# A recurrent decoder trunk on one core: reordering the odd mixer's decay work, and moving four rank products inside their pieces

## The chip, the cores and the metric

The kernel runs on one core of a Trainium2 chip. The metric is the device time of one launch in microseconds (us), as a median over runs.

## The reference, cut to what matters

Two layers; each has a feed-forward half step, a mixer and a second feed-forward half step, for 512 prompt tokens and 8 samples of 8 tokens, all in float32. The even layer's mixer needs low-rank products whose sigmoids give decays. The odd layer's mixer joins a gated linear attention (GLA, "C") and an mLSTM ("D"), both of them chunked:

```python
def _gla(q, k, v, gk, s0):
    bc = jnp.cumsum(gk, -2)
    qd = q * jnp.exp(bc)
    att = jnp.where(causal, jnp.einsum('bnhik,bnhjk->bnhij', qd, k * jnp.exp(-bc)), 0.0)
    intra = jnp.einsum('bnhij,bnhjv->bnhiv', att, v)
    kd = k * jnp.exp(bc[..., -1:, :] - bc)
    # per chunk: o = in_c + qd_c @ s;  s = s * gl_c + kd_c^T v_c

def _mlstm(q, k, v, ig, fg, c0, n0, m0):
    # per chunk, with running maximum m_t:
    #   dm = exp(log_d - m_t) * (q k^T);  num = w_in * (q c) + dm v
    #   h = num / max(|den|, exp(-m_t));  ke = k * exp(log_e - m_new)

def _odd_mixer(h, s_gla, s_c, s_n, s_m, w, i):
    proj = h @ w['w_in_odd'][i]
    o_c = _rms(o_c) * gain_c * silu(z);  o_d = sigmoid(o_in) * _rms(hd) * gain_d
    return concat([o_c, o_d]) @ w['w_out_odd'][i], ...
```

## The kernel before, in words

The program is a sequence of blocks: a dense chain (first feed-forward, even projection), the even mixer, a long dense chain (even output, three feed-forward parts, odd projection), the odd mixer (`odd_mixer`, from L3461 on), and a last dense chain. All five engines run an order that is written out by hand; they meet at semaphores only, and each block ends on all of them before the next one begins.

**Dense chain.** Weights stream in 128-column tiles. Each tile is rounded into a high and a low part (ScalarE at L171, VectorE at L175), and TensorE forms three products per pair of tiles (L1494, L1496, L1498) over `KT` = 8 steps `kt` of the contracted dimension. One tile's worth of that is a piece. In the even projection's pieces numbered 19 to 23, small products for the even mixer are put in between (`even_gates.rank`, L761): after piece 19+i the product `w{i}`, in the middle of piece 20+i (at `kt == KT // 2`) the product `r{i}`. Both write the same PSUM pair, and ScalarE empties it each time with a sigmoid (`decay_rates`, L825): `r{i}` waits for `sig_w{i}`, `w{i+1}` for `sig_r{i}`.

**Odd mixer.** There are four prompt chunks of 128 tokens, 0 to 3, and one chunk of all samples (number 4). For each chunk c, by the names of the steps in `odd_orders` (L3405):

- TensorE: `front` transposes the values (`vct`, `vdt`, L3665), forms key-query products (`qk_0`, `qk_1`) and transposes the mLSTM keys (`kdt`, L3685); `weights` forms the GLA attention (`at_0`, `at_1`, whose 16x16, 32x32 and 64x64 blocks are separate products) and transposes the end-scaled keys (`klt`, L3721); `outputs` forms the outputs (`co`, `do`) and state updates (`sc`, `sd`); `back` transposes the normalised outputs back (`tc`, `td`, L3810). L3650 is the helper that records all plain products.
- ScalarE: `exponents` (L3847 to L3854: `X`, `Xn`, `xl`, `F`); `evict` copies the transposed values (`Vc` L3860, `Vd` L3863) and then computes the decay exponents of the mLSTM (`Lexp`, four at L3872, and `xw`, L3875); `keys` copies `klt` (`KL`, L3880); `square` (L3890) and `roots` (L3895, a square root, which needs another function table than the exponentials, so that ACT_TABLE_LOAD instructions come in between).
- VectorE: `front` (L3925 to L3942), `weights` (`qw` L3959, `DM` L3962, `KE` L3968), `masked` (`AT`, L3981), `sums` (L3996 to L4015), `scaled` (reciprocal L4019, `U` L4026), `gated` (L4062).
- GpSimd: `relative` (`rel`, six subtractions, L3554 and L3555, which `F` needs), `to_the_end` (`te`, L3567, which `xl` needs), `keys_to_end` (`Kl`, L3575), `end_decays` (`eC`, `eD`), and `masked_logs` (`lm`, L3606), which adds a causal mask to the rows of log decays that a DMA broadcast to all partitions; `Lexp` needs it.
- SP: broadcasts of the log rows of chunk 0 (L3514), of the entry rows that `xw` needs (L3517), of the log rows of chunks 1 to 3, each issued only when the one before has landed, then the samples' rows and the 2 MB of GLA and mLSTM states.

PSUM has four fixed banks for outputs and a ring of four for everything else: a job may start only when the fourth job before it in TensorE's order has been read out (`claim`, `odd_release`), so that the order itself sets which step waits for which.

## Time and profile before

| | before |
|---|---|
| median of 3 runs | 2659.85 us (2652.95 to 2662.24) |
| the profiled execution, its own time | 2658.36 us |
| span of its trace | 2656.6 us |
| TensorE busy | 2541.6 us (96%) |
| VectorE / ScalarE / GpSimd busy | 1604.7 / 1057.3 / 650.2 us |
| odd mixer, from 2078.5 to 2188.5 us of the span | 110 us |
| even projection's pieces with rank products, from 570.2 to 608.7 us | 38.5 us |

The span is the trace's own length; the execution's time is 1.8 us more, for what lies around it. Shares of busy time are means over the whole launch, so the odd mixer is read by itself.

### The profile page before, as it was taken

To read this page: it belongs to the slowest core of one execution; us is meant where nothing else is said; L and a number is where in the kernel's file an instruction comes from. 1 tells how busy PE (TensorE), PEld (TensorE's weight loads), DVE (VectorE), ACT (ScalarE), POOL (GpSimd) and SP (SyncE) were. 2 spreads that over 40 slices of the span, in tenths; PEclk is the share of its full clock that TensorE was granted. 3 is DMA by queue.
4 is the path that set the end of the run, shared out by engine and by line. 5 is a ranking of instruction groups with operands and counts; after the bars stand their busy time and mean duration, and the time that the engine had idled before them with its cause. 6 is when DMAs were issued, how large, how long until landed. Compare 5 with 4: busy or idle time off the path is not lost. (4 is left out here: it accounts for less than half of the span.)

```text
span 2656.6 us, 52472 instructions
## 1 busy us (share of the span) xinstructions
PE 2541.6 (96%) x22720; PEld 2389.8 (90%) x22720; DVE 1604.7 (60%) x2302; ACT 1057.3 (40%) x1546; POOL 650.2 (24%) x499
## 2 busy tenths in 40 slices
PE   6999999999999899999999999999999679999998
PEld 4999999888787787999999999999989569999998
DVE  5678726665465555677842677852743356677825
ACT  4444414554344322444432544432432333444513
POOL 0455201000010031155501055500100312355301
PEclk8999999999999979999999999999999789999999
DMA  6332455631000014222255322255751213222324
GB/s 238 104 120 95 157 192 193 236 131 54 29 3 3 9 60 163 64 95 93 93 194 177 121 90 96 96 183 175 234 200 60 76 52 105 66 94 96 101 83 133
DMA packets 82846, 303.30 MB, mean 114 GB/s; under 512 B 9376, under 2 KB 17072, under 8 KB 81336
## 3 DMA queue, kind: packets, MB, share of 16 engines
q1 hardware_dynamic: 82616, 299.95, 34.2%
q8 instruction: 179, 2.93, 0.4%
q14 instruction: 51, 0.42, 0.0%
HBM read 289.16 MB, written 10.76 MB: 113 GB/s over the span
## 5 line engine op out<-in xcount | busy, mean ns | idle before, releaser
L175 DVE TENSOR_TENSOR weights_r<-work,weights_r 128x1024 fp32r<-128x1024 f32 (+2 forms) x309 | 389.6, 1261 | 339.2 <-ACT weights_r L171 339.2
L171 ACT ACTIVATE weights_r<-work 128x1024 fp32r<-128x1024 f32 (+2 forms) x309 | 299.1, 968 | 534.0 <-PE banks L1498 298.9
L1379 POOL TENSOR_TENSOR rows<-rows,consts 128x288 f32<-128x288 f32 (+3 forms) x64 | 82.1, 1282 | 711.8 <-ACT consts L1641 711.8
L1496 PE MATMUL banks<-low_r,weights_r 128*128 128x288 f32 (+1 forms) x1064 | 255.3, 299 | 0.0
L1397 PE MATMUL banks<-big_r,weights_r 128*128 128x288 f32 x768 | 227.0, 296 | 0.0
L1398 PE MATMUL banks<-h_r,weights_r 128*128 128x288 f32 x768 | 226.6, 295 | 0.0
L1396 PE MATMUL banks<-h_r,weights_r 128*128 128x288 f32 x768 | 226.5, 295 | 0.0
L1494 PE MATMUL banks<-h_r,weights_r 128*128 128x288 f32 (+1 forms) x808 | 201.7, 307 | 4.7 <-DVE big_r L437 4.7
L1496 PE MATMUL banks<-big_r,weights_r 128*128 128x288 f32 (+2 forms) x800 | 202.0, 298 | 0.0
L175 DVE TENSOR_TENSOR ring_r<-consts,ring_r 128x1024 fp32r<-128x1024 f32 (+1 forms) x87 | 105.7, 1215 | 153.1 <-ACT ring_r L171 153.1
L1498 PE MATMUL banks<-h_r,weights_r 128*128 128x288 f32 (+1 forms) x808 | 195.3, 299 | 0.0
L1494 PE MATMUL banks<-low_r,weights_r 128*128 128x288 f32 (+2 forms) x720 | 182.1, 302 | 12.0 <-DVE low_r L175 12.0
L1496 PEld LDWEIGHTS banks<-low_r,weights_r 128*128 128x128 f32 x1064 | 181.5, 190 | 0.1
L1498 PE MATMUL banks<-low_r,weights_r 128*128 128x288 f32 (+2 forms) x720 | 178.9, 298 | 0.0
L1396 PE MATMUL banks<-low_r,weights_r 128*128 128x288 f32 x576 | 170.1, 295 | 0.0
L1397 PE MATMUL banks<-low_r,weights_r 128*128 128x288 f32 x576 | 169.9, 295 | 0.0
L1398 PE MATMUL banks<-low_r,weights_r 128*128 128x288 f32 x576 | 169.4, 294 | 0.0
L1494 PEld LDWEIGHTS banks<-h_r,weights_r 128*128 128x128 f32 x808 | 138.0, 190 | 24.3 <-issue 8.9
L171 ACT ACTIVATE ring_r<-consts 128x1024 fp32r<-128x1024 f32 (+1 forms) x87 | 89.6, 1030 | 170.0 <-PE banks L1498 152.4
L1494 PEld LDWEIGHTS banks<-low_r,weights_r 128*128 128x128 f32 x720 | 124.8, 191 | 23.1 <-DVE weights_r L175 13.0
L1398 PEld LDWEIGHTS banks<-h_r,weights_r 128*128 128x128 f32 x768 | 144.9, 189 | 0.0
L1397 PEld LDWEIGHTS banks<-big_r,weights_r 128*128 128x128 f32 x768 | 144.6, 188 | 0.0
(581 smaller groups left out, 7084.9 us busy)
## 6 DMA issues: line engine op xcount, KB each, us to landing
work<-w_ff_dram SPq DMA_DIRECT2D x117, 512.0 KB, 3.6
h<-w_mod_dram SPq DMA_DIRECT2D x48, 768.0 KB, 5.3
consts<-w_ff_dram SPq DMA_DIRECT2D x59, 512.0 KB, 3.6
work<-w_down_dram SPq DMA_DIRECT2D x55, 512.0 KB, 3.5
big_buf<-w_mod_dram SPq DMA_DIRECT2D x24, 768.0 KB, 6.1
consts<-w_down_dram SPq DMA_DIRECT2D x33, 512.0 KB, 3.5
work<-w_down_dram SPq DMA_DIRECT2D x33, 384.0 KB, 3.4
work<-w_mod_first_dram SPq DMA_DIRECT2D x24, 512.0 KB, 12.0
```

What stands on the lines that cost most here:

```text
L171: return act.activation(high, raw, ACT.Copy)
L175: return engine.tensor_tensor(low, raw, high.bitcast(F32), ALU.subtract)
L1379: pool.tensor_tensor(k.rows[:, c], k.rows[:, c], k.square[:, c], ALU.add).then_inc(added, 1)
L1396: pe.matmul(out, low[:, w], x_high, start=j == 0, stop=False)
L1397: pe.matmul(out, high[:, w], x_low, start=False, stop=False)
L1398: last = pe.matmul(out, high[:, w], x_high, start=False, stop=j == KT // 2 - 1)
L1494: pe.matmul(out[a], low[:, w], x[a][0], start=begins, stop=False)
L1496: pe.matmul(out[a], high[:, w], x[a][1], start=False, stop=False)
L1498: last = pe.matmul(out[a], high[:, w], x[a][0], start=False, stop=closes)
```

## The change

It has two parts. In the dense chain the four products `r0` to `r3` move from `kt == 4` to `kt == 6` of their pieces. In the odd mixer:

- ScalarE: `Lexp` and `xw` leave `evict` and become `log_exponents`, which follows `exponents` directly, ahead of `KL`, `root`, `Vc` and `Vd`. At the start `Vc` and `Vd` of chunk 0 come first of all.
- GpSimd: `lm` of a chunk moves from ahead of `rel` (and one chunk early) to behind `te` of its own chunk.
- TensorE: `weights` of chunk 0 moves ahead of `front` of chunk 1.
- VectorE: `masked` of chunk 0 and `front` of chunk 1 come ahead of `weights` of chunk 1.
- SP: each log row has a semaphore of its own, and none is held back for the one before.

```diff
@@ -1471,7 +1471,7 @@
                         for kt in range(lo, hi):
-                            if even_gates and kt == KT // 2 and i in range(even_at(20), even_at(24)):
+                            if even_gates and kt == KT - 2 and i in range(even_at(20), even_at(24)):
                                 even_gates.rank(pe, "r", i - even_at(20))
@@ -3407,7 +3407,8 @@
     front_act = lambda c: pick(c, "X Xn xl F", "X Xn xl")
-    weight_act = lambda c: at(c, ["Vc", "Vd"] + [f"Lexp_{h}" for h in range(2 if c == SAMPLE else 4)] + ["xw"])
+    log_act = lambda c: at(c, [f"Lexp_{h}" for h in range(2 if c == SAMPLE else 4)] + ["xw"])
+    value_act = lambda c: at(c, ["Vc", "Vd"])
     square_act = lambda c: pick(c, "sqC_0 sqC_1 sqD_0 sqD_1", "sqC sqD")
@@ -3417,23 +3418,22 @@
     of = lambda i, names: names(ODD_ORDER[i]) if i < len(ODD_ORDER) else []
-    masks_pool = lambda i: of(i, lambda c: at(c, ["lm"]))
-    pe = of(0, front_pe) + of(1, front_pe) + of(0, weight_pe)
-    act = of(0, front_act) + of(0, weight_act) + of(1, weight_act) + at(ODD_ORDER[0], ["KL"]) + of(1, front_act)
-    dve = of(0, front_dve) + of(0, weight_dve) + of(1, weight_dve) + of(0, masked_dve) + of(1, front_dve)
-    pool = masks_pool(0)
+    pe = of(0, front_pe) + of(0, weight_pe) + of(1, front_pe)
+    act = of(0, value_act) + of(0, front_act) + of(0, log_act) + of(1, front_act) + at(ODD_ORDER[0], ["KL"]) \
+        + of(1, log_act) + of(1, value_act)
+    dve = of(0, front_dve) + of(0, weight_dve) + of(0, masked_dve) + of(1, front_dve) + of(1, weight_dve)
+    pool = []
     for i in places:
         c = ODD_ORDER[i]
-        pool += masks_pool(i + 1)
         if c != SAMPLE:
...
         pe += of_sample(i + 1, "sc0 sc1") + (out_pe(SAMPLE) if of_sample(i + 1, "co") else [])
-        act += square_act(c) + of(i + 2, front_act) + of(i + 1, lambda b: at(b, ["KL"])) + at(c, ["root"]) \
-            + of(i + 2, weight_act)
+        act += square_act(c) + of(i + 2, front_act) + of(i + 2, log_act) + of(i + 1, lambda b: at(b, ["KL"])) \
+            + at(c, ["root"]) + of(i + 2, value_act)
         dve += sums_dve(c) + of(i + 1, masked_dve) + scaled_dve(c) + of(i + 2, front_dve) + of(i + 2, weight_dve)
         dve += of_sample(i, "SC2 SC3 SD2 SD3 SD4 SD5") + gated_dve(c) + of_sample(i + 1, "SC0 SC1 SD0 SD1")
-        pool += pick(c, "rel te Kl eC eD", "te Kl eC eD KEm KLm")
+        pool += pick(c, "rel te lm Kl eC eD", "te lm Kl eC eD KEm KLm")
     return pe, act, dve, pool
@@ -3490,7 +3490,8 @@
         states_in, cleared, n_ready = (ph.sem(x) for x in ("states_in", "cleared", "n_ready"))
-        logs_in, sample_logs_in, entries_in = (ph.sem(x) for x in ("logs_in", "sample_logs_in", "entries_in"))
+        sample_logs_in, entries_in = (ph.sem(x) for x in ("sample_logs_in", "entries_in"))
+        logs_in = [ph.sem(f"logs_in_{c}") for c in range(NCH)]
         log_of = lambda c: log_rows[:, c * 4 * n:(c + 1) * 4 * n].rearrange("p (h i) -> p h i", h=4)
@@ -3511,12 +3512,11 @@
                 def chunk_logs(c):
-                    sp.dma_start(log_of(c), log[None, :, c * n:(c + 1) * n].to_broadcast([P, 4, n])).then_inc(logs_in, 16)
+                    sp.dma_start(log_of(c), log[None, :, c * n:(c + 1) * n].to_broadcast([P, 4, n])).then_inc(logs_in[c], 16)
                 chunk_logs(0)
...
                 for c in range(1, NCH):
-                    sp.wait_ge(logs_in, 16 * c)
                     chunk_logs(c)
@@ -3599,10 +3599,12 @@
                         pool.wait_ge(sample_logs_in, 32)
+                        pool.wait_ge(constants.landed, 32)
                         tt(v2(log_rows_s), v2(log_rows_s), k.half("cut_below8")[:, None, :].to_broadcast([P, 2, m]), ALU.add)\
...
                         return
-                    pool.wait_ge(logs_in, 16 * (c + 1))
+                    pool.wait_ge(logs_in[c], 16)
+                    pool.wait_ge(constants.landed, 32)
                     tt(log_of(c), log_of(c), k.big("cut_below")[:, None, :].to_broadcast([P, 4, n]), ALU.add)\
@@ -3612,15 +3614,12 @@
                 last.then_inc(cleared, 1)
-                pool.wait_ge(constants.landed, 32)
-                masked_logs(ODD_ORDER[0])
                 for i in places:
                     c = ODD_ORDER[i]
-                    if i + 1 < len(ODD_ORDER):
-                        masked_logs(ODD_ORDER[i + 1])
                     if c != SAMPLE:
...
                     to_the_end(c, i)
+                    masked_logs(c)
                     keys_to_end(c, i)
@@ -3813,8 +3812,8 @@
                 front(ODD_ORDER[0])
+                weights(ODD_ORDER[0])
                 front(ODD_ORDER[1])
-                weights(ODD_ORDER[0])
                 for i in places:
@@ -3854,7 +3853,6 @@
                 def evict(c, i):
-                    w = size(c)
                     act.wait_ge(*after("pe", "vct", c))
@@ -3862,6 +3860,9 @@
                         .then_inc(*did("Vd", c))
+
+                def log_exponents(c, i):
+                    w = size(c)
                     act.wait_ge(*after("pool", "lm", c))
@@ -3894,16 +3895,19 @@
 
+                evict(ODD_ORDER[0], 0)
                 exponents(ODD_ORDER[0], 0)
-                evict(ODD_ORDER[0], 0)
+                log_exponents(ODD_ORDER[0], 0)
+                exponents(ODD_ORDER[1], 1)
+                keys(ODD_ORDER[0], 0)
+                log_exponents(ODD_ORDER[1], 1)
                 evict(ODD_ORDER[1], 1)
-                keys(ODD_ORDER[0], 0)
-                exponents(ODD_ORDER[1], 1)
                 for i in places:
...
                         exponents(ODD_ORDER[i + 2], i + 2)
+                        log_exponents(ODD_ORDER[i + 2], i + 2)
                     if i + 1 < len(ODD_ORDER):
@@ -4064,9 +4068,9 @@
                 weights(ODD_ORDER[0], 0)
-                weights(ODD_ORDER[1], 1)
                 masked(ODD_ORDER[0], 0)
                 front(ODD_ORDER[1], 1)
+                weights(ODD_ORDER[1], 1)
                 for i in places:
```

How the orders move, at the three places that matter. First ScalarE in the odd mixer, in the turn of chunk 1 (squares of chunk 1, exponents of chunk 3, key copy of chunk 2, root of chunk 1). Before:

```order
L3847 ACTIVATE work<-big_buf 128x512
L3849 ACTIVATE work<-big_buf 128x256
L3851 ACTIVATE work<-work 128x256
L3854 ACTIVATE work<-work 128x768
L3880 ACTIVATE work<-banks 128x256
L3895 ACT_TABLE_LOAD
L3895 ACTIVATE work<-work 128x8
L3860 ACTIVATE work<-banks 128x512
L3863 ACTIVATE work<-banks 128x4x128
L3872 ACT_TABLE_LOAD
L3872 ACTIVATE work<-work,cols 128x128 x4
L3875 ACTIVATE work<-work 128x256
```

and with the change:

```order
L3846 ACT_TABLE_LOAD
L3846 ACTIVATE work<-big_buf 128x512
L3848 ACTIVATE work<-big_buf 128x256
L3850 ACTIVATE work<-work 128x256
L3853 ACTIVATE work<-work 128x768
L3873 ACTIVATE work<-work,cols 128x128 x4
L3876 ACTIVATE work<-work 128x256
L3881 ACTIVATE work<-banks 128x256
L3896 ACT_TABLE_LOAD
L3896 ACTIVATE work<-work 128x8
L3858 ACTIVATE work<-banks 128x512
L3861 ACTIVATE work<-banks 128x4x128
```

The four `Lexp` and `xw` now stand ahead of the key copy and the root, and the load of the exponential's table has moved from between the root and `Lexp` to ahead of `X`.

Second, TensorE at the start of the odd mixer (`front` is the rows x8, x4, x2; `weights` the five rows on `work` up to 64x64 and the transposes after them). Before:

```order
L3665 MATMUL banks<-base,big_buf 128x128 x8
L3650 MATMUL banks<-big_buf 128x128 x4
L3685 MATMUL banks<-base,big_buf 128x128 x2
L3665 MATMUL banks<-base,big_buf 128x128 x8
L3650 MATMUL banks<-big_buf 128x128 x4
L3685 MATMUL banks<-base,big_buf 128x128 x2
L3650 MATMUL banks<-work 128x128 x4
L3650 MATMUL banks<-work 16x16 x16
L3650 MATMUL banks<-work 32x32 x8
L3650 MATMUL banks<-work 64x64 x4
L3721 MATMUL banks<-base,work 128x128 x2
L3650 MATMUL banks<-work 128x128 x2
```

and with the change:

```order
L3664 MATMUL banks<-base,big_buf 128x128 x8
L3649 MATMUL banks<-big_buf 128x128 x4
L3684 MATMUL banks<-base,big_buf 128x128 x2
L3649 MATMUL banks<-work 128x128 x4
L3649 MATMUL banks<-work 16x16 x16
L3649 MATMUL banks<-work 32x32 x8
L3649 MATMUL banks<-work 64x64 x4
L3720 MATMUL banks<-base,work 128x128 x2
L3664 MATMUL banks<-base,big_buf 128x128 x8
L3649 MATMUL banks<-big_buf 128x128 x4
L3684 MATMUL banks<-base,big_buf 128x128 x2
L3649 MATMUL banks<-work 128x128 x2
```

`weights` of chunk 0 now stands between the two fronts.

Third, TensorE in the even projection, the last of the four pieces with an `r` product (L761). Before:

```order
L1498 MATMUL banks<-h_r,weights_r 128x300 x2
L761 MATMUL banks<-big_buf,work 128x288 x2
L1494 MATMUL banks<-h_r,weights_r 128x300 x2
L1496 MATMUL banks<-low_r,weights_r 128x300 x2
L1498 MATMUL banks<-h_r,weights_r 128x300 x2
L1494 MATMUL banks<-h_r,weights_r 128x300 x2
L1496 MATMUL banks<-low_r,weights_r 128x300 x2
L1498 MATMUL banks<-h_r,weights_r 128x300 x2
L1494 MATMUL banks<-h_r,weights_r 128x300 x2
L1496 MATMUL banks<-low_r,weights_r 128x300 x2
```

and with the change:

```order
L1498 MATMUL banks<-h_r,weights_r 128x300 x2
L1494 MATMUL banks<-h_r,weights_r 128x300 x2
L1496 MATMUL banks<-low_r,weights_r 128x300 x2
L1498 MATMUL banks<-h_r,weights_r 128x300 x2
L1494 MATMUL banks<-h_r,weights_r 128x300 x2
L1496 MATMUL banks<-low_r,weights_r 128x300 x2
L1498 MATMUL banks<-h_r,weights_r 128x300 x2
L761 MATMUL banks<-big_buf,work 128x288 x2
L1494 MATMUL banks<-h_r,weights_r 128x300 x2
L1496 MATMUL banks<-low_r,weights_r 128x300 x2
```

The product stands two steps of `kt` (three products for two sides each) later in its piece.

## Rows read from the trace of the kernel before

**Rows 1.** The page: busy time, share of the span and instructions of the engines.

```profile
PE 2541.6 (96%) x22720; PEld 2389.8 (90%) x22720; DVE 1604.7 (60%) x2302; ACT 1057.3 (40%) x1546; POOL 650.2 (24%) x499
```

**Rows 2.** Waits, 569 to 612 us: engine, line, waited for; us in total, times, longest.

```profile
PE banks L761 <- ACT work L825: 4.3, 4, 1.1
```

**Rows 3.** Timeline, TensorE and ScalarE around `r0` and `w1`: start, us, engine, instruction, idle before.

```profile
575.19 0.74 ACT L825 ACTIVATE work<-banks,params 128x576 f32<-128x576 f32 x1
575.98 1.24 PE L761 MATMUL banks<-big_buf,work 64*128 64x288 f32 x4 [1.08 <-ACT work L825]
577.25 0.74 ACT L825 ACTIVATE work<-banks,params 128x576 f32<-128x576 f32 x1 [1.32 <-PE banks L761]
...
580.64 1.23 PE L761 MATMUL banks<-big_buf,work 64*128 64x288 f32 x4
```

**Rows 4.** Timeline, start of the odd mixer (begins at 2078.5 us).

```profile
2080.47 1.50 PE L3665 MATMUL banks<-base,big_buf 128*128 128x128 f32 x8 [4.04 <-DMA consts<-consts_in_dram]
...
2083.94 1.09 POOL L3606 TENSOR_TENSOR work<-work,consts 128x512 f32<-128x512 f32 x1 [2.89 <-DMA work<-decay_rows]
...
2088.71 0.40 POOL L3554 TENSOR_TENSOR work<-big_buf 128x128 f32<-128x128 f32 x1
...
2090.88 0.61 POOL L3567 TENSOR_TENSOR work<-big_buf 128x256 f32<-128x256 f32 x1
...
2092.57 0.58 ACT L3860 ACTIVATE work<-banks 128x512 f32<-128x512 f32 x1
...
2098.77 0.40 ACT L3875 ACTIVATE work<-work 128x256 f32<-128x256 f32 x1
...
2100.16 2.54 PE L3650 MATMUL banks<-work 64*128 64x128 f32 x64 [1.31 <-DVE work L3962]
...
2103.36 0.38 ACT L3880 ACTIVATE work<-banks 128x256 f32<-128x256 f32 x1 [4.19 <-PE banks L3721]
...
2103.84 1.19 PE L3650 MATMUL banks<-work 128*128 128x128 f32 x4 [0.52 <-DVE work L3981]
```

**Rows 5.** Timeline, SP's issue of the two entry rows (L3517).

```profile
2078.89 1.28 SPq L3517 DMA_DIRECT2D work<-decay_rows  x2
```

**Rows 6.** DMA issues, 2076 to 2100 us: KB of one, us from issue to landing.

```profile
work<-decay_rows SPq DMA_DIRECT2D x2, 288.0 KB, 5.7
...
work<-mn_in_dram SPq DMA_DIRECT2D x1, 8.0 KB, 8.4
```

**Rows 7.** Stretches: length, busy us of PE, PEld, DVE, ACT, POOL, clock, DMA share, GB/s.

```profile
2114.00:2118.00 4.00, 3.45 (x80) 2.74 (x76) 2.26 (x7) 2.00 (x4) 0.86 (x2) 0.86 0.01 4
```

```profile
2152.00:2153.00 1.00, 1.00 (x49) 0.78 (x48) 1.00 (x3) 0.00 (x0) 0.00 (x0) 0.66 0.00 0
```

**Rows 8.** Timeline, the turn of chunk 1, from the end of its squares to `td`.

```profile
2131.59 0.63 ACT L3847 ACTIVATE work<-big_buf 128x512 f32<-128x512 f32 x1
...
2132.72 0.84 ACT L3854 ACTIVATE work<-work 128x768 f32<-128x768 f32 x1
...
2134.63 0.38 ACT L3880 ACTIVATE work<-banks 128x256 f32<-128x256 f32 x1 [1.07 <-PE banks L3721]
...
2135.03 1.28 ACT L3895 ACT_TABLE_LOAD   x1
...
2138.82 1.28 ACT L3872 ACTIVATE work<-work,cols 128x128 f32<-128x128 f32 x4
...
2140.78 0.75 DVE L3962 SCALAR_TENSOR_TENSOR work<-banks,work 128x256 f32<-128x256 f32 x2
...
2141.34 1.09 PE L3810 MATMUL banks<-base,work 128*128 128x128 f32 x4 [3.07 <-DVE work L3962]
```

**Rows 9.** Timeline, ScalarE: key copies in the turns of chunks 0 and 2, root of chunk 3.

```profile
2115.97 0.38 ACT L3880 ACTIVATE work<-banks 128x256 f32<-128x256 f32 x1 [2.00 <-PE banks L3721]
...
2154.08 0.39 ACT L3880 ACTIVATE work<-banks 128x256 f32<-128x256 f32 x1 [3.02 <-PE banks L3721]
...
2166.64 0.21 ACT L3895 ACTIVATE work<-work 128x8 f32<-128x8 f32 x1 [0.92 <-DVE work L4015]
```

## The prediction

> **What bounds the kernel now.** First the page: TensorE is busy 96% of the span [rows 1], so time can only be won where TensorE idles or runs slowly. Neither edit removes a product. Next the waits of the stretch that each edit touches, then the timeline around them. In the even projection TensorE waits four times for a sigmoid of ScalarE, 4.3 us in all [rows 2]. In the odd mixer it idles between short bursts, and the stretches show the rest: the granted clock is at its lower level (0.50, 1.2 GHz against 2.4) until about 2115 us, and again in the turn of chunk 2 until 2152.7 (the 0.86 and 0.66 are means over a stretch with the change in it) [rows 7]. I read that part as a chain over all engines.
>
> **Even projection.** `r0` starts at 575.98 after 1.08 us of idling, right behind `sig_w0` (575.19 + 0.74 = 575.93); it would have been reached at 574.90 [rows 3]. From the end of `r0` (577.22) to `w1` (580.64) four steps of `kt` take 3.4 us, so two take 1.7, and `r0` is now reached at 576.6, 0.7 after the sigmoid. The wait goes: 4 x 1.07 = **-4.3 us** [rows 2]. A new wait could arise at `w1`, which needs `sig_r0`: that starts 1.27 after `r0` and takes 0.74 [rows 3], so it ends at 578.6, and `w1` comes at 576.6 + 1.24 + 1.7 = 579.5. With 0.9 us to spare it costs nothing. TensorE has no other wait there. Bounds: 0, if `w` waited as long as `r` did, and -4.3.
>
> **Start of the odd mixer.** Before, GpSimd waits 2.89 us for the first log row, masks it (1.09 us), then waits for and masks the second, and comes to `rel` only at 2088.71; `te` ends at 2091.49 [rows 4]. `xl` and `F`, the copies behind them and all of TensorE's work stand behind that; `at` of chunk 0 starts at 2100.16 and the first output product at 2103.84 [rows 4]. The new order, step by step:
>
> - `vct` and `vdt` end at 2081.97 (2080.47 + 1.50). `Vc` and `Vd`, 0.58 each, end at about 2082.6 [rows 4]. A table load of 1.28 follows, to 2083.9; `X` to `F` take 1.97 (2131.59 to 2133.56), to 2085.9 [rows 8].
> - `rel` and `te` take 2.78 (2088.71 to 2091.49). GpSimd is free at 2081.05, where its wait of 2.89 began, so `te` ends at 2083.8, in time for `xl`. The log row is there at 2083.94 and `lm` ends at 2085.0 [rows 4], in time for `Lexp`.
> - `Lexp` and `xw` take 1.28 + 0.40 less an overlap of 0.1, 1.6 in all [rows 4, 8], to 2087.5. The entry rows that `xw` needs are issued from 2078.89 and land 5.7 us after each issue, by about 2085.3 [rows 5, 6].
> - `at` followed the end of `xw` (2099.17) by 1.0 [rows 4]; it still does, through `DM`, which must empty a bank that `at_1` now claims. `at` starts at 2088.5.
> - `klt` was ready 3.2 after that start and `KL` 3.6 [rows 4]; so `klt` is ready at 2091.7. ScalarE first has `X` to `F` of chunk 1, whose `rel` and `te` start after `xw`: 2087.8 + 2.8 = 2090.6, `xl` and `F` to 2092.0, `KL` to 2092.4, `Lexp` and `xw` to 2094.0, `Vc` to 2094.5.
> - TensorE's front of chunk 1 is 1.5 for the transposes and 1.2 for `qk`, since four output products of that size take 1.19 at this clock [rows 4]: to 2094.4. `kdt`, half as many, waits for `Vc` and takes 0.6; outputs start at 2095.0.
>
> That is 2103.84 - 2095.0 = **-8.8 us**. Bounds: -5, if a wait of the size of those removed (2.9) and 0.9 of smaller ones come back, and -9.5. The four log rows now leave at once, ahead of 2 MB of states. I count nothing for that: the 8 KB row that was issued last, behind those 2 MB, took 8.4 us to land [rows 6], so later transfers queue behind earlier ones.
>
> **The turns.** In chunk 1's turn ScalarE goes from the squares through `X` to `F` (2133.56), waits 1.07 for `klt`, copies `KL`, loads the table and takes the root [rows 8]. Now a load (1.28) stands ahead of `X` and `Lexp` with `xw` (1.6) behind `F`: 2131.59 + 1.28 + 1.97 + 1.6 = 2136.4, against 2134.63: `KL` and the root come 1.8 later. Nothing is won behind the root: `xw` ended at about 2140.4 and `DM`, after a multiply of 0.4, started at 2140.78 [rows 4, 8], so VectorE came to it no earlier; it was busy from the root on. `td` waits for `DM` (3.07 idle) and the next outputs for `td` [rows 8], so this is on the path: **+1.8 us**. In chunk 0's turn there is no load ahead, and the 1.6 fit in ScalarE's 2.00 of idling; in chunk 2's the load and the half-size exponents, 1.28 + 0.8, fit in 3.02 [rows 9]. The root of chunk 3 waited for VectorE (0.92 idle), so the load that disappears there was hidden [rows 9]. Bounds: 0 if `klt` were later anyway, +5.4 if all three turns paid.
>
> Here a rule speaks for more. Rows first: a load takes 1.28 us and the next instruction follows at once [rows 8]. The Trainium skill, "ScalarE: Activation LUTs", *What ACT_TABLE_LOAD costs*, gives 1.28 plus a drain, 2.66 in all, and its *Table sets: the hidden batching unit* advises finishing one set before switching. The order has two loads fewer (8 to 6), which by that rule is -5.3 us; by rows it is nothing, since both removed loads were hidden.
>
> **Sum.** -4.3 - 8.8 - 1.4 + 1.8 = -12.7 us, so 2658.4 becomes 2645.7. The profiled execution is 1.5 below the median of its kernel, and for the median I forecast **2647 us**. A difference of 0.3% is 8 us; below that a measurement of this kernel tells nothing from no change.
>
> **Rivals.**
>
> - *Loads saved count.* By counting sets the two loads are 2 x 1.28 = 2.6 us more: 2644.5. For it: the order has them; against: ScalarE idles 3.02 and 0.92 where they stood [rows 9]. Chance 0.04. (The Trainium skill's batching rule, above, is this case.)
> - *Every turn pays.* If the clock's earlier return takes ScalarE's idling away, the turns of chunks 0 and 2 pay 1.8 too: +3.6, 2650.7. For it: only 0.4 to spare in one. Against: an earlier `klt` is itself a gain. Chance 0.08.
> - *The start gives half.* Some step that I have not seen, as a copy in ScalarE's order or a bank, takes up 3.8, and the clock comes back no earlier: -4.3 - 5 + 1.8 = -7.5, 2652.4. For it: ten steps in a row had to fit. Chance 0.10.
> - *Slower: the first log row is buried.* If transfers that are issued together share the engines evenly, the first log row and the entry rows land with the last. All in all they are 3.7 MB. The two 288 KB rows took 6.4 us (90 GB/s, with their latency), the last 2 MB of states 8.4 us (240 GB/s) [rows 5, 6]; at 160, between them, it is 23 us, landing near 2101.5. From there `lm`, `Lexp`, `xw` and on to the outputs are 1.1 + 1.6 + 1.0 + 6.5 = 10.2: outputs at 2111.7, +7.9. With -4.3 and +1.8: 2665.3. It decides from the point where that row lands after 2096. Against it: the 8.4 us [rows 6]. The Trainium skill, "DMA: Bandwidth & Descriptors", *Queues, rings and completion order*, says that each engine takes descriptors in ring order though completions may cross; with that the trace agrees. Chance 0.03.
> - *The change doesn't do what it says in the even part.* `w` inherits the wait: -8.4, 2651.5. Against: 0.9 us to spare. Chance 0.03.
>
> **How the numbers follow.** The forecast has 0.72. Its bounds run from -4.3 - 9.5 - 2.6 = -16.4 to -4.3 - 5 + 1.8 = -7.5, so 2643.5 to 2652.4; with 2 us of scatter on each side the range is 2641 to 2654.5, and it holds all rivals but the slower one. Faster by over 0.3%: 0.67 of the forecast, 0.04, 0.05 of the turns, 0.02 of the last, 0.78 in all. Within 0.3%: 0.05 of the forecast, 0.03, 0.10, 0.01, together 0.19. Slower: 0.03.
>
> **What would show it.** Right: no wait of TensorE at the rank products; outputs of chunk 0 near 16.5 us after the mixer's start, not 25.4; the clock back before 25 us; the root of chunk 1 6.5 us after the squares, not 4.7; the mixer 8 us shorter. Wrong: `xw` of chunk 0 waiting for a DMA, a new wait ahead of `kdt` or `at` of over 1 us, or the same mixer length with an earlier start, which would mean that a turn takes it back.

## The result, and the profile after

The changed kernel takes 2641.6 us (median of 6 runs, 2635.5 to 2643.8). The kernel before, run on the same occasions, takes 2654.1 (6 runs, 2651.1 to 2662.2). The ratio is 0.9946, with a 95% interval of 0.9927 to 0.9965: faster by 9 to 19 us, and in the middle by 14. The forecast was 2647 with a gain of 12.7.

The profiled executions differ by more, 2658.4 against 2641.6, since that of before lies 4.3 us above the median of its six runs and that of after lies on its own. The ledger below is of this pair. "Mixer" is the odd mixer, from its first memset (2078.46 before, 2073.90 after) to the first copy of the next dense chain (2188.53, 2171.38).

| stretch, us | before | after | change | forecast |
|---|---|---|---|---|
| `w0` to the even mixer's first product | 154.19 | 149.57 | -4.6 | -4.3 |
| mixer's start to first output product | 25.38 | 16.44 | -8.9 | -8.8 |
| first output to root of chunk 0 | 13.82 | 9.82 | -4.0 | -1.4 |
| root of chunk 0 to root of chunk 1 | 18.66 | 18.34 | -0.3 | +1.8 |
| root of chunk 1 to root of chunk 2 | 19.46 | 18.48 | -1.0 | 0 |
| root of chunk 2 to root of chunk 3 | 10.86 | 10.86 | 0 | 0 |
| root of chunk 3 to the mixer's end | 21.89 | 23.54 | +1.7 | 0 |
| the mixer | 110.07 | 97.48 | -12.6 | -8.4 |

The two blocks that were worked out in detail came as forecast. The rest of the mixer did not, and what is in it is the subject of the experiments. Below, turn 1 is the step from root of chunk 0 to root of chunk 1, and turn 2 the next one; each begins with the rest of the chunk before, up to its `td`.

The page's first part, which answers to [rows 1]:

```profile
PE 2534.6 (96%) x22720; PEld 2384.8 (90%) x22720; DVE 1604.1 (61%) x2302; ACT 1054.2 (40%) x1544; POOL 650.6 (25%) x499
```

TensorE has as many products as before and is busy 7.0 us less, since more of them ran at the higher clock; its idling (the span less the busy time) shrank from 115.0 to 105.3 us. ScalarE has two instructions fewer, the two table loads.

The timeline of the even projection, which answers to [rows 3] (columns as there):

```profile
575.44 0.74 ACT L825 ACTIVATE work<-banks,params 128x576 f32<-128x576 f32 x1
576.75 1.24 PE L761 MATMUL banks<-big_buf,work 64*128 64x288 f32 x4
578.02 0.74 ACT L825 ACTIVATE work<-banks,params 128x576 f32<-128x576 f32 x1 [1.83 <-PE banks L761]
579.74 1.24 PE L761 MATMUL banks<-big_buf,work 64*128 64x288 f32 x4
```

`sig_w0` ends at 576.18 and `r0` starts at 576.75 with no wait. `sig_r0` ends at 578.76 and `w1` starts at 579.74: the new spare time is 1.0 us (0.9 was reckoned), and `w` inherits nothing. From `w0` to `w1` a period is 9.33 us instead of 10.49.

The start of the odd mixer, which answers to [rows 4]:

```profile
2077.99 0.60 ACT L3861 ACTIVATE work<-banks 128x512 f32<-128x512 f32 x1 [0.26 <-PE banks L3664]
2078.61 1.28 ACT L3846 ACT_TABLE_LOAD   x1
2078.61 0.62 POOL L3567 TENSOR_TENSOR work<-big_buf 128x256 f32<-128x256 f32 x1
2079.18 1.10 POOL L3608 TENSOR_TENSOR work<-work,consts 128x512 f32<-128x512 f32 x1
...
2081.78 1.26 ACT L3873 ACTIVATE work<-work,cols 128x128 f32<-128x128 f32 x4
2082.95 0.40 ACT L3876 ACTIVATE work<-work 128x256 f32<-128x256 f32 x1
2084.29 2.54 PE L3649 MATMUL banks<-work 64*128 64x128 f32 x64 [4.55 <-ACT work L3848]
...
2090.34 0.61 PE L3649 MATMUL banks<-work 128*128 128x128 f32 x4
```

GpSimd goes from `te` to `lm` without waiting for the log row (L3608 at 2079.18, 5.3 after the start), and ScalarE goes through exponents and `xw` without waiting either. So the first log row wasn't buried behind the states, and `at` starts 10.4 after the mixer's start (forecast 10.0). The first output products take 0.61, not 1.19 as in [rows 4]: they already run at the higher clock.

The stretches say when it came back, and when it fell again. Columns: length, busy us of PE, PEld, DVE, ACT, POOL, then the granted clock, DMA share, GB/s.

```profile
2086.00:2088.00 2.00, 2.00 (x26) 1.82 (x19) 1.14 (x4) 1.37 (x4) 2.00 (x4) 0.50 1.01 303
2088.00:2090.00 2.00, 1.49 (x14) 1.12 (x12) 2.00 (x7) 2.00 (x8) 1.08 (x3) 0.91 0.54 147
2090.00:2094.00 4.00, 3.94 (x30) 3.16 (x30) 1.70 (x6) 1.15 (x4) 3.56 (x8) 1.00 0.01 0
...
2107.00:2109.00 2.00, 2.00 (x11) 1.55 (x12) 0.00 (x0) 0.00 (x0) 1.30 (x2) 0.54 0.00 0
2109.00:2112.00 3.00, 3.00 (x32) 2.39 (x34) 0.00 (x0) 1.17 (x4) 0.00 (x0) 1.00 0.00 0
...
2150.00:2152.00 2.00, 2.00 (x16) 1.67 (x17) 1.33 (x2) 0.00 (x0) 0.00 (x0) 0.50 0.22 41
```

The 2 us from 2088 are a mean of 0.91: 0.36 us of them were still at half the clock, so the change from 1.2 to 2.4 GHz lies at 2088.4, 14.5 after the mixer's start and 4.1 after the start of `at`. Before it was 36.7 and 15.0. In the turns the lower level returns: in turn 1 for 6.8 us, where before it stayed for 10.2, and in turn 2 for 13.7 in both. The last row is in the sample's outputs, where the clock was low for 3.4 us; before it wasn't: that is the +1.7 of the table.

The turn of chunk 1, which answers to [rows 8]:

```profile
2112.17 1.28 ACT L3846 ACT_TABLE_LOAD   x1
2114.01 0.44 PE L3720 MATMUL banks<-base,work 128*128 128x128 f32 x2
2116.52 0.40 ACT L3876 ACTIVATE work<-work 128x256 f32<-128x256 f32 x1
2116.82 0.36 ACT L3881 ACTIVATE work<-banks 128x256 f32<-128x256 f32 x1
2117.20 1.28 ACT L3896 ACT_TABLE_LOAD   x1
2118.50 0.21 ACT L3896 ACTIVATE work<-work 128x8 f32<-128x8 f32 x1
...
2123.42 1.09 PE L3809 MATMUL banks<-base,work 128*128 128x128 f32 x4 [2.51 <-DVE work L3966]
```

ScalarE now doesn't wait in front of the key copy (L3881). `klt` ended at 2114.45 and the copy came 2.4 after it, where before it came at once. The root comes 6.3 after the squares' end (load at 2112.17), as forecast. Yet the step from root to root didn't grow.

### The profile page after: what moved, and what is told of

It is laid out like the page before. It is cut to its first block and busy times, and to the rows that moved or that the text cites. A ratio compares the mean times of both kernels' runs of the same rounds, so it can differ in the third digit from the quotient of the medians.

```text
span 2639.9 us, 52474 instructions
## 1 busy us (share of the span) xinstructions
PE 2534.6 (96%) x22720; PEld 2384.8 (90%) x22720; DVE 1604.1 (61%) x2302; ACT 1054.2 (40%) x1544; POOL 650.6 (25%) x499
## 5 line engine op out<-in xcount | busy, mean ns | idle before, releaser
L1494 PEld LDWEIGHTS banks<-h_r,weights_r 128*128 128x128 f32 x808 | 138.9, 192 | 24.2 <-issue 8.9
```

What stands on the lines that cost most here:

```text
L1494: pe.matmul(out[a], low[:, w], x[a][0], start=begins, stop=False)
```

## The experiments

Two theories stood at the outset. **A**, the forecast's: the gain is the sum of two independent parts, the start of the mixer and the rank products, and the early exponents cost something in the turns. **B**: what the mixer gained beyond its start is not the order but the clock, which can fall differently from one execution to the next. Rivals for single steps are given with the runs. All ratios are against the kernel before on the same chip; roots are those of chunks 0, 1 and 2, in us from the mixer's start (before: 39.2, 57.9, 77.3; after: 26.3, 44.6, 63.1). The mixer's own length is read beside the ratio, since what lies ahead of it scatters: in the kernels below that have the new even part the mixer begins between 2065.2 and 2076.8 us.

### One part at a time

On the kernel before, the rank products alone (the kernel is called e1 here, and so on by the numbers of the labels):

```diff
-                            if even_gates and kt == KT // 2 and i in range(even_at(20), even_at(24)):
+                            if even_gates and kt == KT - 2 and i in range(even_at(20), even_at(24)):
```

> Only the four r products move from kt 4 to kt 6; the odd mixer is as before. My theory: TensorE's four waits of 1.07 us behind ScalarE's sigmoid go and nothing takes their place, so the even mixer begins 4.3 us earlier and the launch is 4.3 us shorter (ratio 0.9984). Rival: part of the even gain is handed back where the clock or a DMA decides later, so that the time does not move (ratio 1.000) although the even mixer begins 4.3 us earlier.

Measured: ratio 0.9987 (0.9973 to 1.0002), 2652.8 us; `w0` to the even mixer 149.58 instead of 154.19, as in the changed kernel; mixer 109.87, roots 37.3, 56.9, 75.5. The interval holds 1, so the time alone doesn't show this gain; the trace does. The unchanged mixer shows how far its start varies: the first output comes at 24.0 instead of 25.4, because GpSimd waits 2.11 and 2.02 us for its two log rows and not 2.89 and 2.64.

The changed kernel with `KT // 2` put back, so the odd mixer alone:

> Only the odd mixer's reordering, the rank products as before. Theory: the mixer is 12.6 us shorter than before (97.5 against 110.1 us), as in the changed kernel, and the launch 8 to 13 us shorter (ratio 0.995 to 0.997). Rival: the odd mixer's gain in the changed kernel's profile depends on where its clock changes happened to fall, and with the mixer shifted by 4.3 us it is only the 9 us of the start (mixer 101 us).

Measured: 0.9965 (0.9949 to 0.9981), 2645.4 us; `w0` to the even mixer 154.27; mixer 99.05; first output at 16.34, roots 26.2, 46.5, 66.2. The two ratios give 0.9952 together, against 0.9946 for both: within their intervals the parts add up. The mixer is 1.6 longer than the changed kernel's with the same order in it. Its two turns are 3.2 longer (in turn 1 its clock was low for 13.7 us, the other's for 6.8), and its last step, from root of chunk 3 on, is 1.6 shorter, because the clock didn't fall in its sample's outputs. In e2, `KL` comes 0.7 behind the end of `klt`, in the profile of after 2.4. So turn 1's -0.3 in the ledger is a loss to the exponents and a gain of the clock on top of each other.

### What the early exponents cost in the turns

The changed kernel, with exponents and `xw` of the turns behind the root again and only those of the start early:

```diff
-        act += square_act(c) + of(i + 2, front_act) + of(i + 2, log_act) + of(i + 1, lambda b: at(b, ["KL"])) \
-            + at(c, ["root"]) + of(i + 2, value_act)
+        act += square_act(c) + of(i + 2, front_act) + of(i + 1, lambda b: at(b, ["KL"])) \
+            + at(c, ["root"]) + of(i + 2, value_act) + of(i + 2, log_act)
...
```

(ScalarE's calls of `log_exponents` move in the same way.)

> The changed kernel, but with Lexp and xw of the chunk two ahead behind the root and the value copies again in the turns (the start keeps its new order). Theory (my term for the turns): the early exponents and the table load ahead of X delay KL and the root; without them the root of chunk 1 comes 2.4 us earlier behind klt, and that of chunk 0 about 1 us earlier, so the mixer is 2 to 3.5 us shorter than the changed kernel's 97.5 (about 94.5). Rival: td waits for VectorE's DM, which then waits for the late Lexp, so nothing is won or the mixer is up to 1 us longer.

Measured: 0.9934 (0.9911 to 0.9957), 2637.4 us; mixer 96.69; roots 25.5, 44.4, 63.9. In the timeline of this kernel the key copy follows `klt` at once again, and the root follows the copy by 1.3:

```profile
2117.68 0.44 PE L3720 MATMUL banks<-base,work 128*128 128x128 f32 x2
2118.15 0.39 ACT L3881 ACTIVATE work<-banks 128x256 f32<-128x256 f32 x1 [1.34 <-PE banks L3720]
...
2119.85 0.21 ACT L3896 ACTIVATE work<-work 128x8 f32<-128x8 f32 x1
```

From first output to root of chunk 0 it takes 9.11, where the changed kernel takes 9.82: 0.7 in a turn for which 0 was forecast. For the other turns only those may be compared in which the clock is low equally long and at the same place. With 13.7 us of it that begin 3.1 to 3.7 after the root of chunk 0, turn 1 takes 20.3 with early exponents (20.31 in e2; 20.28 to 20.29 in three more profiles below) and 19.56 in e1, which has them late: 0.75. (In e12, further below, with late exponents, the 13.7 us begin 0.7 after the root, and turn 1 takes 18.6: the place counts.) Turn 2 takes 19.5 to 19.75 in four profiles with early exponents against 19.44 to 19.49 in four with late ones, where the low stretch begins 0.3 to 1.3 us sooner after the root: at most 0.3, and perhaps nothing. Together 1.5 to 1.8 us, spread over three turns, where 1.8 was forecast for one. The ratios of e3 and of the changed kernel overlap, so the total time alone wouldn't tell.

### Is it the clock in the turns?

In the kernel before, the clock falls 2.4 us and 0.8 us into the two waits of 3.1 us for `DM` ahead of `td` [rows 8]. In the changed kernel ten products of the identity with itself, into a bank whose content is overwritten later, fill that wait; nothing reads them.

```diff
+                        if job == "td" and c < NCH - 1:
+                            for _ in range(10):
+                                mm(bank("do_1", c)[:, 0:P], ident, ident)
```

> The changed kernel with ten products of the identity by itself between tc and td of chunks 0 to 2 (they write a bank that has been read out; their result is not used), which fill about 2.7 of the 3 us in which TensorE waits for DM. Theory: that idling is what takes the clock down; with it filled the granted clock stays at 1.00 through the outputs of chunks 1 and 2, which then take about 4.2 us and not 5 to 8, and the mixer is 5 to 8 us shorter than the changed kernel's 97.5. Rival: the clock falls for another reason (a lighter load of the small transposes and waits before it), then the outputs take as long as before and the time does not move, or grows by up to 1 us where the products delay td.

Measured: 0.9928 (0.9906 to 0.9951), 2637.8 us; mixer 94.34; roots 26.3, 43.9, 59.3; the clock low twice for 3.4 us in the turns, 6.8 in all instead of 20.5. TensorE in chunk 0's turn (ends of products are modelled):

```profile
2093.41 4.10 PE L3649 MATMUL banks<-base 128*128 128x128 f32 x20
2097.34 0.60 PE L3812 MATMUL banks<-base,work 128*128 128x128 f32 x4
```

The ten took 3.9 us to `td`, partly at the lower level, longer than the wait they fill, and held `td` back by 0.9 (32.1 after the mixer's start, not 31.2). Turn 1 went from 18.3 to 17.6 and turn 2 from 18.5 to 15.4. The step behind them, from root of chunk 2 to root of chunk 3, grew from 10.9 to 13.1.

That the clock still fell twice says something on the cause. Turn 2 in the profile of after, then in e4:

```profile
2114.00:2118.00 4.00, 2.21 (x22) 1.61 (x18) 1.31 (x5) 3.98 (x11) 1.78 (x5) 1.00 0.00 0
2118.00:2122.00 4.00, 1.72 (x8) 1.00 (x6) 3.23 (x12) 1.67 (x4) 0.00 (x0) 0.64 0.00 0
```

```profile
2105.00:2109.00 4.00, 1.80 (x16) 1.16 (x14) 0.85 (x4) 3.98 (x9) 1.78 (x5) 1.00 0.00 0
2109.00:2113.00 4.00, 3.05 (x15) 2.85 (x16) 3.67 (x14) 1.23 (x4) 0.00 (x0) 0.68 0.00 0
```

In after the 0.64 puts the fall at 2119.1, while the wait for `DM` begins only at 2120.9; in e4 the 0.68 puts it at 2110.4, 0.8 ahead of the ten products. What stands ahead of the fall in both is shorter idling, of 1.6 and 1.2 us, for copies by ScalarE that the early exponents delay. In turn 1 both clocks fell just as the wait or the ten products began (28.1 and 28.2 after the start), behind 1.2 us of idling. So in these two profiles the wait for `DM` isn't what took the clock down; but with it filled the clock came back sooner (low for 6.8 and 13.7 us in after, for 3.4 and 3.4 in e4).

The same with seven products, on the kernel of e3, so that neither too long a fill nor the exponents are in the way:

> The start of the changed kernel, Lexp and xw in the turns behind the root as before, and seven identity products (not ten, which took 3.9 us and held td back by 0.9) between tc and td of chunks 0 to 2; their result is not used. Theory: both gains add up where the clock stays up, because ScalarE's early exponents cost most (2.3 us behind klt) when TensorE is quick: root of chunk 1 about 16.5 us after the root of chunk 0 and not 18.3, the mixer 91 to 93 us. Rival: VectorE or the late exponents bound the turn once TensorE is quick, and the mixer stays at 94 or above.

Measured: 0.9923 (0.9906 to 0.9939), 2633.9 us; mixer 89.52; roots 25.2, 39.6, 53.9. Both turns take 14.36, to 0.01. The timeline and the stretch:

```profile
2099.16 0.21 ACT L3899 ACTIVATE work<-work 128x8 f32<-128x8 f32 x1
2101.11 1.83 PE L3649 MATMUL banks<-base 128*128 128x128 f32 x14
2104.09 0.66 PE L3812 MATMUL banks<-base,work 128*128 128x128 f32 x4 [1.14 <-DVE work L3969]
...
2113.52 0.21 ACT L3899 ACTIVATE work<-work 128x8 f32<-128x8 f32 x1
```

```profile
2099.00:2128.00 29.00, 25.17 (x332) 19.71 (x330) 19.57 (x60) 16.89 (x40) 6.86 (x16) 1.00 0.00 1
```

Seven products of 1.83 us end well ahead of `td`, and the clock stays at 1.00 through both turns. The two turns are 9.7 us shorter than in e3, the mixer 7.2. Of the rest, 1.6 go back in the next step, from the root of chunk 2 to that of chunk 3 (12.47 instead of 10.86), and 1.2 in the last, where the clock fell for 3.4 us behind the root of chunk 3. The run times don't separate e7 from e3: their ratios overlap, and the medians differ by 3.5 us.

Does that hold without the change? The kernel before, with the same seven products and nothing else:

> The kernel before, with seven identity products (unused result) between tc and td of chunks 0 to 2 and nothing else. Theory: the 3 us in which TensorE waits for DM take the clock down, independently of the change; the turns of chunks 1 and 2 then go from root to root in about 14.4 us as in the changed start with filled turns, not 18.7 and 19.5, and the mixer is 8 to 9 us shorter than before's 110.1. Rival: the turns' speed rests on the change (GpSimd's rel and te, or Lexp early), then root to root stays over 16.

Measured: 0.9968 (0.9950 to 0.9985), 2649.8 us; mixer 100.78 (110.07 without them); roots 37.7, 52.1, 66.4, so turns of 14.37 and 14.36:

```profile
2129.00:2143.00 14.00, 12.13 (x162) 9.35 (x161) 9.79 (x30) 7.39 (x18) 1.40 (x4) 1.00 0.01 1
```

The turns' length is the same to 0.01 us in both kernels when the clock holds. Both have the exponents behind the root, so this says that the new start and GpSimd's new order change nothing in the turns; early exponents with the clock up through both turns were not run. The kernel before lost 9.4 us to the clock there (38.1 us for the two turns, now 28.7), and the change did nothing about it.

The step from root of chunk 2 to root of chunk 3 takes 12.47 here too, though the clock is at 1.00 all through it. The seven products do that themselves: in chunk 2's turn `td` comes right behind `tc` in the kernel before, with no wait to fill, and here `tc` and `td` are 2.3 apart:

```profile
2144.65 0.66 PE L3813 MATMUL banks<-base,work 128*128 128x128 f32 x4 [1.13 <-DVE work L4029]
...
2146.98 0.60 PE L3813 MATMUL banks<-base,work 128*128 128x128 f32 x4
```

A kernel with products in the turns of chunks 0 and 1 alone was not run; by this row it should save these 1.6 us, an estimate.

### What part of the start is which

The start has two causes in it: GpSimd's masks stood ahead of `rel` and `te`, and ScalarE's exponents and TensorE's `weights` came late. Here only the first is undone: masks first, one chunk ahead, and log rows issued one after another.

```diff
                 for i in places:
                     c = ODD_ORDER[i]
+                    if i + 1 < len(ODD_ORDER):
+                        masked_logs(ODD_ORDER[i + 1])
                     if c != SAMPLE:
...
                     to_the_end(c, i)
-                    masked_logs(c)
                     keys_to_end(c, i)
```

(with `masked_logs(ODD_ORDER[0])` ahead of the loop, and `sp.wait_ge(logs_in[c - 1], 16)` ahead of `chunk_logs(c)`)

> The changed kernel with GpSimd's masks (lm) of chunks 0 and 1 again ahead of the first rel, the later ones again one chunk early, and the log rows again broadcast one after another; the orders of ScalarE, TensorE and VectorE stay changed. Theory: rel and te then wait for the second log row as before (te ends 13.0 us after the mixer's start, not 5.3), and at of chunk 0 starts at 16.7 and not at 10.4; the mixer grows by 5 to 6.5 us to about 103.5. Rival: the start was won by the orders of ScalarE and TensorE, and at starts at 12 or earlier, the mixer under 100.

Measured: 0.9985 (0.9967 to 1.0003), 2649.6 us; mixer 106.07, which begins at 2074.90; `at` at 16.6 where 10.4 stands in the changed kernel; roots 33.5, 53.8, 73.3. The cause in its timeline:

```profile
2080.28 1.09 POOL L3610 TENSOR_TENSOR work<-work,consts 128x512 f32<-128x512 f32 x1 [2.79 <-DMA work<-decay_rows]
2084.09 1.09 POOL L3610 TENSOR_TENSOR work<-work,consts 128x512 f32<-128x512 f32 x1 [2.73 <-DMA work<-decay_rows]
```

Twice GpSimd stands for a row of logs with `rel` and `te` behind it. That is 6.2 of the 11.3 us by which `at` moved (21.7 to 10.4); the orders of the other engines are the other 5.1 (3.7 if `at` of the old order is taken from e1, where the rows landed earlier and it came at 20.3). The interval of the ratio holds 1, so this too is read from the trace. The log rows' own issue is a separate matter: the changed kernel with the serial issue alone,

```diff
                 for c in range(1, NCH):
+                    sp.wait_ge(logs_in[c - 1], 16)
                     chunk_logs(c)
```

> The changed kernel with the log rows again broadcast one after another by SP, all else as changed. Theory: nothing changes, since lm of chunk 1 starts 12.7 us after the mixer's start and the second row is there by about 9.3: at of chunk 0 at 10.4 us and the first outputs at 16.4. Rival: the early issue matters (a row comes late), then outputs start at 17.5 or later.

Measured (one execution): 2646.6 us, mixer 99.47, `at` at 10.8, first output at 16.97, roots 26.8, 47.1, 66.7. In that profile SP issues the later rows slowly, and chunk 0 doesn't care:

```profile
2083.01 6.74 SPq L3515 DMA_DIRECT2D work<-decay_rows  x3
...
2087.66 2.55 PE L3650 MATMUL banks<-work 64*128 64x128 f32 x64 [4.91 <-DVE work L3967]
```

The 0.5 us at `at` is small beside the 6.2, and 0.4 of it is there already at TensorE's first transposes (2.5 after the start, not 2.1), so the early issue gives nothing that is seen here. The longer turns are those of e2.

### The clock behind the start

"First output to root of chunk 0" shrank by 4.0 where 1.4 was forecast. If that is the clock, then the kernel before must show it once TensorE is kept busy ahead of its late start. A first attempt put 18 identity products ahead of `kdt` in `front` of chunk 0:

```diff
+                    if c == ODD_ORDER[0]:
+                        for _ in range(18):
+                            mm(bank("do_1", c)[:, 0:P], ident, ident)
```

> The kernel before, with eighteen identity products (unused result) in TensorE's idle time after the first key-query products (10 us), and nothing else. Theory: in the changed kernel 3.5 to 4 us of the gain come from the clock being back when the outputs of chunk 0 run, as distinct from the 9 us of the start; filling before's idle time gives that part alone: outputs of chunk 0 still start at 25.4 us, but the root of chunk 0 comes at 34.5 to 35.5 and not at 39.2. Rival: the clock stays low until the outputs are over, whatever ran before, and the root comes at 39 as before.

Measured: 1.0007 (0.9987 to 1.0027); mixer 111.82, root of chunk 0 at 39.4. It decides nothing, as the timeline and the stretch show:

```profile
2087.57 4.60 PE L3650 MATMUL banks<-base 128*128 128x128 f32 x36
...
2097.34 0.69 PE L3688 MATMUL banks<-base,big_buf 128*128 128x128 f32 x2 [5.16 <-ACT work L3863]
```

```profile
2108.00:2116.00 8.00, 8.00 (x38) 6.20 (x40) 3.74 (x9) 2.81 (x8) 5.18 (x11) 0.50 0.00 1
```

The products ran for the most part at the higher clock, were done early, and left 5.2 us of idling; 2.9 us into it the clock fell to its lower level and stayed there until 36.7, as in the kernel before. With 37 products there and 4 more ahead of `weights(0)`:

> The kernel before, with 37 identity products (unused result) in the idle time after the first key-query products and four more ahead of at, so that TensorE has work nearly without a break until the outputs; the eighteen of the last try ran at the high clock, took 4.6 us and left 5.2 idle, after which the clock fell again and the root of chunk 0 came at 39.4. Theory: now the clock is up when the outputs of chunk 0 run, they take about 4 us and not 7.5, and the root of chunk 0 comes 4 to 5 us earlier, at 34.5 to 35.5 us after the mixer's start. Rival: outputs run at the low clock whatever ran before, root at 39 as before.

Measured: 0.9976 (0.9959 to 0.9993), 2651.8 us; mixer 106.59; first output at 24.2 and root of chunk 0 at 34.1, 9.9 later, where the kernel before takes 13.8 and the changed one 9.8.

```profile
2074.18 9.60 PE L3650 MATMUL banks<-base 128*128 128x128 f32 x74
...
2093.11 0.68 PE L3650 MATMUL banks<-work 128*128 128x128 f32 x4 [0.52 <-DVE work L3986]
```

The output products take 0.68 instead of 1.19 and the turn is 3.9 shorter, in the old order. So the 3.9 is the clock. What in the changed order brings it back so early is not shown: it isn't less idling ahead of `at`, since e5 idles 11.2 us there and still has the clock back at 23.0, before its first output at 23.7. The rest cancels: at the high clock the turn takes 9.9 in the old order (e12), 9.1 in the new one (e3) and 9.8 with the exponents early, so -0.8 for the order and +0.7 for the exponents.

### How late the rank products may come, and a faster kernel

The changed kernel with `kt == KT - 1`:

> The changed kernel with the four r products at kt 7 and not 6. By my margin: r is reached 0.86 us later, its sigmoid ends 0.86 later, and w had 0.9 to spare (it comes 1.7 us less 0.74 after the sigmoid's start), so w just does not wait or waits under 0.2 us; from the first w product to the even mixer it takes 149.6 us as with kt 6, at most 150.2. Rival: w inherits the wait, 150.5 or more.

Measured (one execution, 2645.2 us): `w0` to the even mixer 149.65 (149.57 at `KT - 2`). The rows of `r0`, its sigmoid and `w1`:

```profile
577.58 1.24 PE L761 MATMUL banks<-big_buf,work 64*128 64x288 f32 x4
578.85 0.74 ACT L825 ACTIVATE work<-banks,params 128x576 f32<-128x576 f32 x1 [2.65 <-PE banks L761]
579.79 1.24 PE L761 MATMUL banks<-big_buf,work 64*128 64x288 f32 x4
```

The sigmoid ends at 579.59, 0.2 before `w1`: one step later in the piece is the last that is free, and the margin reckoned in the prediction (0.9 less one step's 0.85) was right.

Last, the kernel of e7 with the start improved: the table load, `X` and `Xn` of chunk 0 ahead of `Vc` and `Vd`, and eight identity products in the idling ahead of `weights(0)`.

```diff
-    act = of(0, value_act) + of(0, front_act) + of(0, log_act) + of(1, front_act) + at(ODD_ORDER[0], ["KL"]) \
+    act = at(ODD_ORDER[0], ["X", "Xn"]) + of(0, value_act) + at(ODD_ORDER[0], ["xl", "F"]) + of(0, log_act) + of(1, front_act) + at(ODD_ORDER[0], ["KL"]) \
...
                 front(ODD_ORDER[0])
+                for _ in range(8):
+                    mm(bank("do_1", ODD_ORDER[0])[:, 0:P], ident, ident)
                 weights(ODD_ORDER[0])
...
```

(ScalarE's calls move in the same way.)

> As the kernel with turns filled by seven products, and the start tuned too: ScalarE loads its table and computes X and Xn of chunk 0 before the copies Vc and Vd, and TensorE runs eight identity products (unused result) while it waits for the first DM. Theory: xw of chunk 0 ends 1.3 us earlier (8.1 instead of 9.4 us after the mixer's start), at starts at 9.1, and the clock may be back before the outputs; the mixer is 1.3 to 3 us shorter than the one without this. Rival: the first log row's landing decides (at 5.3 us, lm 1.1, Lexp and xw 1.6), so that the gain is under 1 us, or the eight products at the low clock delay at.

Measured: 0.9905 (0.9883 to 0.9927), 2632.0 us (2622.7 to 2635.3), the lowest ratio measured; mixer 88.84, first output at 15.15. It starts at 2075.66, and its start reads:

```profile
2081.02 2.23 PE L3649 MATMUL banks<-base 128*128 128x128 f32 x16
2083.47 0.40 ACT L3883 ACTIVATE work<-work 128x256 f32<-128x256 f32 x1
2084.91 1.66 PE L3649 MATMUL banks<-work 64*128 64x128 f32 x64 [1.66 <-DVE work L3972]
```

`at` comes 9.25 after the start and takes 1.66 instead of 2.54, since the clock is up: it was low only from 2.5 to 5.9 after the start, in e7 to 16.2. The first output is 1.1 earlier than in e7, but the mixer only 0.7 shorter. That is below what the run times tell apart: the ratios of e7 and e8 overlap.

## Why the prediction was right or wrong

The total, -12.7, is inside the interval, and the time, 2641.6, is inside the range but near its lower edge. The step that failed is the term for the clock behind the start: its mechanism was right, its size was not (-1.4 forecast, -4.0 measured). The 5.4 us between time and forecast come from elsewhere: the runs of before had a median of 2654.1 in place of the 2659.9 on which the forecast stood, 5.8 less. Taken against that median, 2647 would have been a gain of 7.1 us, half of what was measured.

That -12.7 came so near is luck in part. In the ledger the clock behind the start gave 2.6 more than forecast and the turns 3.1, and 1.7 went back at the end; e2, with the same mixer, had neither of the last two: its turns are 1.9 us longer than those of before, near the forecast's 1.8, and its last step is the same. By its steps:

- **Even projection, -4.3: right.** -4.6 in the pair and in e1 alike. The extra 0.3 is that a period also loses the small gap around the wait (1.16 instead of 1.08, four times). The bound of 0 and the rival "`w` inherits the wait" fall with e11, where `w` has 0.2 left even one step later.
- **Start of the mixer, -8.8: right,** -8.9, with `at` at 10.4 (10.0) and the outputs at 16.4 (16.5). That is against the profiled execution; the first output of the unchanged start lay at 24.0 in e1 and e9 and at 25.7 in e10, which makes it 7.5 to 9.2. e5 splits the earlier `at` into 6.2 for GpSimd's masks and 5.1 for the other orders. "I count nothing" for the log rows that leave at once was right, too (e6). The slower rival, a buried log row, falls with the profile of after: no wait at `lm` or `xw`.
- **The clock behind it, -1.4: mis-sized, and the step that failed.** "14.9 after the start of `at`" was carried over from before. After the change it was 4.1, in the other changed orders 4.2 to 6.8; in the old order it was 13.4 to 15.0 (e1, e9, e10, before). The clock was back at 14.5, not at 21.3 to 24.9. So all of the step from first output to root of chunk 0 ran at the higher level, worth -4.0 in the ledger and -3.9 in e12, more than the bound of -2.6. The "40%" was right (13.8 against 9.9 in e12), but it was applied to a return only 2.9 to 6.5 us earlier. That TensorE then works almost without a break was right.
- **The turns, +1.8: the size was right, the places were wrong.** At equal clock the early exponents cost 0.7, 0.75 and at most 0.3 (e3, e1, e2), 1.5 to 1.8 in all. The prediction put 1.8 on chunk 1 and let chunk 0 hide it in 2.00 of idling [rows 9]; that row was read at the slow clock. With the clock up `klt` came sooner and the cover was gone, which is the rival "every turn pays", in part. The ledger shows -0.3 and -1.0 nonetheless, since in this pair the clock was low for 6.8 us in turn 1, not 10.2, and in turn 2 its 13.7 us began 0.6 after the root, not 2.7, so that less of the work behind it ran slowly. That gain is not the change's: e2, with the same order in the mixer, didn't have it.
- **Loads saved, 0: right.** e3 has all eight loads back and isn't slower. The Trainium skill, "ScalarE: Activation LUTs", *Table sets: the hidden batching unit*, advises finishing a set before switching; here the order that batches less was no slower. By the timelines the loads that went stood in idle time, and the one moved ahead of `X` stands in front of a key copy that others wait for. The figure of 2.66 us with a drain, from *What ACT_TABLE_LOAD costs* on the same page, isn't borne out: the load takes 1.28, and the root follows at 2118.50, 0.02 after its end.
- **Left out altogether:** the clock's fall in the turns. The prediction names one low stretch, up to 2152.7 [rows 7], and takes it as given; it doesn't name the other, of 10.2 us from 2122.0. The two turns lost 9.4 us by them in the kernel before (e9) and 9.7 with the new start (e3 to e7), about as much as the start gave. Also left out was the fall in the sample's outputs, +1.7 in this pair. It is none of the change's either: six of the fourteen profiles have it, of old orders (e1, e10, e12) and new ones (after, e7, e8).

## What to carry to other kernels

Take an engine's wait for data first with what stands behind it on its own queue: 3 us of GpSimd waiting for a row that only a later step needs held up four engines. In a chain of short bursts look at the granted clock before the order: where TensorE idles a few us between dependent bursts, a few unused products that end before the data comes can be worth as much as a reordering (9.4 us in two turns here, 8.9 for the new start). Their number has to be fitted to the wait (ten were too many here, seven fitted, eighteen of them in one place were too few), and where there is no wait they only cost (seven took 1.6 us in chunk 2's turn). And where idling hides a cost, ask at which clock that idling was measured.

## What the runs showed of the hardware

- The time to return to the higher clock differs a lot for like work: 4.1 to 6.8 us after the start of `at` in the changed orders, 13.4 to 15.0 in the old one. In turn 1 the clock was low for 6.8 us in after and for 13.7 in e2, which have the same mixer. What sets it stays open; no run here separates it.
- Each profile with waits of TensorE of 2.5 to 3.1 us in these turns had the clock low in both turns. In most the clock fell within the wait; in after (turn 2; in turn 1 just as the wait began) and in e12 (turn 1) it had fallen before, behind idling of 1.2 to 1.6 us, and in e4 it fell with the wait filled. With late exponents and 1.83 us of products in the wait it stayed at 1.00 over both turns (e7 and e8, and e9 in the old order).
- One and the same wait can go either way: 2.5 us of idling ahead of the transposes behind the root of chunk 3 stand in all fourteen profiles, and the clock fell within 1.8 us of their end in six of them. Where it did, the step from that root to the mixer's end took 23.2 to 23.6 us, elsewhere 21.9 to 22.0.
- One of the six runs of e4 took 4258.5 us, with a mean granted clock of 0.656 where the others had 0.974 to 0.979. The others lie between 2629.7 and 2639.2, and the ratio is theirs. No profile shows the long one; its cause stays open.
